# Hyena's three-tap convolution inside the input projection's evictions instead of inside attention

## The reference

```python
def centred_conv3(x, w, b):
    return shift_prev(x) * w[0] + x * w[1] + shift_next(x) * w[2] + b

def hyena(u, sw, sb, ...):
    u = centred_conv3(u, sw, sb)              # per sequence, zero at its ends
    v, x1, x2 = jnp.split(u, 3, axis=-1)
    z = v
    for o, gate in enumerate((x1, x2)):
        conv = ...                            # long convolution with kernel o, by Fourier transforms
        z = gate * (conv + skip[o] * z)
    return z

p = h @ w_in                                  # 3 * 512 columns q, k, v, then 3 * 512 for Hyena
y = concat([attention(q, k, v, kc, vc, rpb), hyena(p[..., 3 * A:], ...)]) @ w_out
```

## Time and profile before

| | us |
|---|---|
| median of 3 runs | 2537.68 (2536.79 to 2539.23) |
| profiled execution, first to last instruction | 2542.4 |
| of it, PE busy | 2305.5 |
| DVE, ACT, POOL busy | 946.4, 664.9, 864.1 |
| first eviction of a Hyena tile to the last (starts) | 194.27 to 315.55 |
| first scores of attention to the last store | 318.67 to 438.05 |

### The profile page before, as it was taken

One profiled execution on the slowest core, in us unless ns is written; L12 is line 12 of the kernel. 1 busy time (PEld: TensorE's weight loads), 2 busy tenths in 40 slices (PEclk: granted clock), 3 DMA queues, 4 the chain that ended last, 5 costly groups with the idle time before them and its releaser, 6 DMA issues. The chain is left out here.

```text
span 2542.4 us, 50323 instructions
## 1 busy us (share of the span) xinstructions
PE 2305.5 (91%) x22240; PEld 1932.1 (76%) x22240; DVE 946.4 (37%) x1475; ACT 664.9 (26%) x1031; POOL 864.1 (34%) x699
## 2 busy tenths in 40 slices
PE   5899976998889999999958998999999987999997
PEld 3787854555479999999927987888888865888785
DVE  3110066793130000022288214677777633000123
ACT  4110065431240000022132123444444223111112
POOL 2222200000224343434306444333333233666562
PEclk8999997998889999999979999999999988999998
DMA  6555520001111212111112343222221112323221
GB/s 255 199 215 199 198 92 18 0 1 58 42 42 59 66 58 66 58 60 65 48 50 69 107 145 86 42 44 42 42 42 40 23 59 83 99 91 99 87 96 67
DMA packets 139266, 204.06 MB, mean 80 GB/s; under 512 B 87783, under 2 KB 97511, under 8 KB 131912
## 3 DMA queue, kind: packets, MB, share of 16 engines
q1 hardware_dynamic: 139080, 201.26, 25.1%
HBM read 183.93 MB, written 17.30 MB: 79 GB/s over the span
## 5 line engine op out<-in xcount | busy, mean ns | idle before, releaser
L258 POOL CAST TMP_r<-WR 128x1024 fp32r<-128x1024 f32 x120 | 126.5, 1054 | 730.2 <-DMA WR<-in_ffn_w_dram 438.3
L277 PE MATMUL PS<-H_r,TMP_r 128*128 128x384 f32 (+1 forms) x1088 | 330.6, 359 | 10.9 <-DVE Y_r L494 10.9
L277 PE MATMUL PS<-Y_r,TMP_r 128*128 128x384 f32 (+1 forms) x1088 | 330.2, 358 | 3.7 <-DVE H_r L494 3.7
L260 POOL TENSOR_TENSOR WR_r<-WR,TMP_r 128x1024 fp32r<-128x1024 f32 x120 | 289.2, 2410 | 9.6
L417 DVE TENSOR_TENSOR P<-TMP,PS 128x768 f32 (+1 forms) x44 | 36.1, 821 | 562.8 <-PE PS L277 562.8
L277 PEld LDWEIGHTS PS<-H_r,TMP_r 128*128 128x128 f32 x1088 | 202.7, 190 | 27.4 <-DVE Y_r L494 11.6
L277 PEld LDWEIGHTS PS<-Y_r,TMP_r 128*128 128x128 f32 x1088 | 201.7, 190 | 19.3 <-DVE H_r L494 4.0
L277 PE MATMUL PS<-H_r,WR_r 128*128 128x384 f32 x736 | 191.9, 342 | 0.0
L400 ACT ACTIVATE TMP<-PS 128x768 f32<-128x768 f32 (+1 forms) x44 | 31.0, 705 | 526.3 <-PE PS L277 526.3
L594 PE MATMUL PS<-H_r,TMP_r 128*128 128x384 f32 x704 | 151.9, 338 | 3.2 <-DVE H_r L632 2.2
L277 PE MATMUL PS<-Y_r,WR_r 128*128 128x512 f32 x352 | 139.4, 396 | 0.0
(11 more groups left out here) (321 smaller groups left out, 4526.1 us busy)
## 6 DMA issues: line engine op xcount, KB each, us to landing
WR<-in_ffn_w_dram SPq DMA_DIRECT2D x88, 512.0 KB, 3.6
TMP<-in_mod_w_dram SPq DMA_DIRECT2D x40, 1024.0 KB, 4.9
WR<-in_down_dram SPq DMA_DIRECT2D x44, 512.0 KB, 3.5
WR<-in_mix_w_in_dram SPq DMA_DIRECT2D x24, 512.0 KB, 7.0
WR<-in_rw_w_rkv_dram SPq DMA_DIRECT2D x24, 512.0 KB, 4.2
P<-in_mod_w_dram SPq DMA_DIRECT2D x4, 2048.0 KB, 21.8
vkr_dram<-extra SPq DMA_DIRECT2D x16, 384.0 KB, 4.8
scan_front<-vkr_dram SPq DMA_DIRECT2D x16, 384.0 KB, 4.2
```

The lines of the kernel that those rows point to most:

```text
L258: nc.gpsimd.tensor_copy(hi, raw).then_inc(weights_hi, 1)
L260: nc.gpsimd.tensor_tensor(lo, raw, hi.bitcast(F32), ALU.subtract).then_inc(weights_split, 1)
L277: last = nc.tensor.matmul(PS[:, bank + b, 0:h1 - h0], w, x[:, h0:h1], start=k + p == 0, stop=k == CT - 1 and p == 2)
```

## The change

The taps are applied where a Hyena tile leaves PSUM. ACT's eviction of tile t (12 to 23) becomes scale by the middle weight plus bias, and counts `conv3_begun`. DVE then adds the left tap and the right tap, reading the neighbours from the PSUM banks, that is the values before any tap, and adding in place to tile t of `P`. The two halves of 384 columns and the border at column 512 cut each tap into three instructions. Only after the second tap does DVE count `inproj.unit_free`. Nothing of the convolution is left in attention or Hyena. The convolved tiles now lie at 12 to 23, so Hyena reads `P[:, HY + ...]` with HY = 12, and `WAVES` moves to tiles 0 to 11.

Two orders change besides. On DVE, `inproj_dve` interleaves the convolutions with the modulation columns. On PE, the scores of steps 0 and 1 begin as soon as bank pairs 0 and 1 are free of their last tiles, and the last turn of the modulation follows them.

```diff
@@ attn_pe
+            for u in range(2):
+                pe.wait_ge(inproj.unit_free, IN_TILES - IN_UNITS + u + 1)
+                scores(u)
+            mod_turn_pe(pe, NMOD - 1)
             pe.wait_ge(inproj.unit_free, inproj.done)
-            scores(0)
-            scores(1)
             pe.wait_ge(mod_added, NMOD)
...
@@ attn_act
-            def conv3_begin(i, j):
-
-                act.wait_ge(scores_done, 2 * (6 * i + 6))
-                act.wait_ge(v_done, 3 * i + 3)
-                nc.scalar.activation(P[:, 4 * j + i, :], P[:, 12 + 4 * j + i, :], ACT.Identity,
-                                     scale=col(SW_COL + 12 + 4 * j + i), bias=col(SB_COL + 4 * j + i))\
-                  .then_inc(conv3_begun, 1)
...
-                if u >= 6 and u % 6 < 3:
-                    conv3_begin(u // 6 - 1, u % 6)
             out(STEPS - 1)
-            for j in range(3):
-                conv3_begin(PAIRS - 1, j)
...
-        def conv3_dve(v, i, j):
-            src, dst = P[:, 12 + 4 * j + i, :], P[:, 4 * j + i, :]
-            for step, (begun, n) in enumerate(((conv3_begun, 3 * i + j + 1), (conv3_step, 3 * i + j + 1))):
-                v.wait_ge(begun, n)
-                for s0, s1, _ in segs():
-                    here, there = (slice(s0 + 1, s1), slice(s0, s1 - 1))[::1 if step == 0 else -1]
-                    ins = nc.vector.scalar_tensor_tensor(dst[:, here], src[:, there],
-                                                         col(SW_COL + 24 * step + 4 * j + i), dst[:, here],
+        def conv3_dve(v, t):
+
+            b = 2 * (t % IN_UNITS)
+            raw = P[:, t, :]
+            steps = (((0, 0, HALF, 1), (1, 0, L - HALF - 1, HALF + 1), (1, L - HALF, HALF - 1, L + 1)),
+                     ((0, 1, HALF, 0), (1, 0, L - HALF, HALF - 1), (1, L - HALF + 1, HALF, L)))
+            for step, parts in enumerate(steps):
+                if step == 0:
+                    v.wait_ge(conv3_begun, t - 11)
+                else:
+                    v.wait_ge(conv3_step, t - 11)
+                for bank, c0, c1, at in parts:
+                    dst = raw[:, at:at + c1 - c0]
+                    ins = nc.vector.scalar_tensor_tensor(dst, PS[:, b + bank, c0:c1], col(SW_COL + 24 * step + t - 12), dst,
                                                          ALU.mult, ALU.add)
-                ins.then_inc(conv3_done if step else conv3_step, 1)
+                ins.then_inc(inproj.unit_free if step else conv3_step, 1)
+
+        def inproj_dve(v, chain):
+            for i in range(2):
+                network_dve(v, chain, 0, i)
+            for g in range(1, 3):
+                mod_cols_dve(v, g)
+                network_dve(v, chain, 1, g - 1)
+            for t in range(12, 17):
+                conv3_dve(v, t)
+            mod_cols_dve(v, 3)
+            for t in range(17, 21):
+                conv3_dve(v, t)
+            mod_cols_dve(v, 4)
+            for t in range(21, IN_TILES):
+                conv3_dve(v, t)
+            mod_cols_dve(v, 5)
...
@@ attn_dve
-                if u >= 6 and u % 6 < 3:
-                    conv3_dve(v, u // 6 - 1, u % 6)
-            conv3_dve(v, PAIRS - 1, 0)
...
-        WAVES, EARLY, LATER = Pf[:, 12 * T:24 * T], WRf, Hraw[:, 4 * T:8 * T]
+        WAVES, EARLY, LATER = Pf[:, 0:12 * T], WRf, Hraw[:, 4 * T:8 * T]
+        HY = 12
...
@@ hyena_pe
             pe.wait_ge(attn_out, STEPS)
-            pe.wait_ge(conv3_done, 10)
             filters(0, 1, 0)
...
@@ hyena_dve
-            v.wait_ge(conv3_done, 10)
-            conv3_dve(v, PAIRS - 1, 1)
             filtered(0, 1, 0)
             filtered(0, 3, 4)
             filtered(0, 0, 2)
-            conv3_dve(v, PAIRS - 1, 2)
             filtered(1, 1, 2)
...
@@ inproj_pe
-            mod_turn_pe(pe, NMOD - 1)
...
@@ inproj_act
-                    nc.scalar.activation(as_halves(P[:, t, :]), halves(b), ACT.Copy).then_inc(inproj.unit_free, 1)
+                    nc.scalar.activation(as_halves(P[:, t, :]), halves(b), ACT.Identity, scale=col(SW_COL + t),
+                                         bias=col(SB_COL + t - 12)).then_inc(conv3_begun, 1)
```

More of the change, by code:

```diff
@@ L691, in hybrid_dit_kernel @@
         conv3_step = sem("conv3_step")
-        conv3_done = sem("conv3_done")
         def latent(u):
@@ L1079, in turn @@
                         pe.wait_ge(HDV.sem, HDV[f"z{r - 2}.{c}"])
-                    last = nc.tensor.transpose(PS[:, bank, 128 * c:128 * c + 128], P[:, c, at:at + 255:2], ident[:, :])
+                    last = nc.tensor.transpose(PS[:, bank, 128 * c:128 * c + 128], P[:, HY + c, at:at + 255:2], ident[:, :])
                 HPE.done(last, f"zt{r}.{k}")
@@ L1426, in gated @@
                 v.wait_ge(HAC.sem, HAC[f"sc{r}.{c}"])
-                tmp, z = scaled_of(r, c), P[:, c, first:first + n]
+                tmp, z = scaled_of(r, c), P[:, HY + c, first:first + n]
                 HDV.done(nc.vector.scalar_tensor_tensor(tmp, z, col(SKIP_COL + 4 * o + c), tmp, ALU.mult, ALU.add),
@@ L1431, in gated @@
                 HDV.done(nc.vector.tensor_tensor(z if o == 0 else H[:, 4 + c, first:first + n], tmp,
-                                                 P[:, 4 + 4 * o + c, first:first + n], ALU.mult), f"z{r}.{c}")
+                                                 P[:, HY + 4 + 4 * o + c, first:first + n], ALU.mult), f"z{r}.{c}")
             def product(r, f):
                 products(nc.vector, HDV, v, r, f, slice(0, HW))
-            v.wait_ge(conv3_done, 10)
-            conv3_dve(v, PAIRS - 1, 1)
             filtered(0, 1, 0)
@@ L3041, in _ @@
                            early=lambda t: Y[:, t, :])
-            for i in range(2):
-                network_dve(v, chain, 0, i)
-            for g in range(1, NMOD):
-                mod_cols_dve(v, g)
-                if g < 3:
-                    network_dve(v, chain, 1, g - 1)
+            inproj_dve(v, chain)
             attn_dve(v)
```

## The result

The changed kernel takes 2500.33 us (median of 4 runs, 2493.22 to 2507.65); the kernel before 2537.23 us (4 runs, 2534.24 to 2539.23: the three above and one more). The ratio is 0.9855, 95% interval 0.9837 to 0.9872: 36.9 us less, where 35.1 were forecast, and 2500.3 us where 2502.6 were. The profiled execution of the changed kernel took 2497.23 us, with a span of 2495.4.

What follows compares the result with a forecast made beforehand. The prediction took PE (91% busy) as the bound, with waits in attention's convolution loops. Savings of 27.9 + 1.4 + 3.3 + 2.7, less 0.2, gave 35.1 us: 2537.7 to 2502.6 us, range 2496 to 2517.

Steps and rivals of the forecast that it cites:

- Part 1: Attention without the convolution: two pairs of heads at 20.0 us each and three loops at 9.1, together 27.9 us saved.
- sixth kind of step: Attention step with queries, scores and values but no batch of values, hidden behind a convolution before; taken as 3.45 us.
- floor of 18.0: Lower bound in us for a pair of heads in attention, from PE's own work, busy 90% in the first pair.
- Part 2: Last three steps of attention: full instead of half clock, 5.0 us in place of 6.4, 1.4 us saved.
- Part 3: From attention to Hyena: PE's filters wait only for the last store, not the tenth convolution; 3.3 us saved.
- Part 4: First Hyena filters: 2.7 us saved if full clock holds through the hand-over, 0 if not.
- Part 5: Input projection: 2.9 us of DVE taps per tile stay hidden; attention's start loses some 0.2 us.
- A: Rival, chance 0.1: attention runs into PE at half clock, each such pair losing 9 us; one gives 2512 us.
- B: Rival, chance 0.06: GpSimd and DVE exclude each other in the projection, and the turn into attention is slow; 2511 us.
- D: Rival, chance 0.02: the convolution in attention was hidden and other waits replace it; 2532 us.
- C: Rival, chance 0.03: evictions hold PE back in the projection from 19.2 us per tile, slower than before from 23 us.
- hidden five times over: Projection: a tile's bank pair is free after some 4.1 us, while PE wants it back only after 19.2 us.

Runs made afterwards that it cites:

- e2: The kernel before with all twelve convolutions left out (wrong result): 2504.40 us, ratio 0.9869.
- e5: The kernel before without ACT's twelve begins of the convolution, DVE's taps left where they are (wrong result): 2510.68 us, ratio 0.9894.
- e9: The changed kernel with three unused ACT instructions put behind attention's last store, PE's filters waiting for them: 2509.24 us in one run.
- e3: The changed kernel without DVE's taps, ACT's eviction freeing the banks: 2501.82 us, ratio 0.9852.
- e6: The changed kernel with the taps reading a tile in SBUF instead of the PSUM banks (wrong result): 2498.42 us in one run.

## Why the prediction was right, step by step

- **Part 1** carries most of the sum and held: pairs of 19.88 and 19.89 us against 20.0, three loops of 9.01 against 9.1, together 28.2 against 27.9. e2 shows that the conv, and nothing else in the change, is its cause. The sixth kind of step, which the trace of before could not show, takes 3.3 us where 3.45 was taken. The warning not to multiply 4.03 by the loops was right, and e5 gives the size: 3.09 us a loop. The floor of 18.0 was too low: the stretch from 335.42 on, from which it was read, holds 158 matmuls and begins at no store, a pair has 170, and PE's work of a pair is 18.34 us. So the pairs stand 1.5 us above their floor.
- **Part 2** had the right mechanism and a wrong size: 3.90 us where 5.0 was taken, 2.5 saved in place of 1.4. At clock 1.00 PE is busy 3.30 of 4.18 us up to the filters, so ACT and DVE end fewer waits than assumed. e2 and e5 support the cause: with gaps of 0.40 and 1.66 us ahead of these steps in place of 3.37 the clock is 1.00.
- **Part 3** held to 0.1 us.
- **Part 4** held in size (2.7). Its reason was incomplete: it makes the 2.7 us depend on whether the clock stays up through the hand-over, and does not see that part 3 removes a gap that brings it down. e9 shows that this gap is enough by itself. Both it and the idle loops were removed, so the sum did not notice; that is luck.
- **Part 5**: taps 2.57 us a tile against 2.9 (the six durations do add up to 2.87; on the engine they overlap a little), ACT 0.99, nothing lost to them (e3). The exclusion was judged rightly from lines 417 and 632 (21 of line 417's 22 instructions of 512 elements ran beside a split, and each took 0.69 us), and e6 shows both sides of it. The 0.2 us at the start lies below what can be told there.
- **Rivals.** A fell: the clock is 1.00 in each pair. Its price of 9 us a pair was too low: the same 38 matmuls kept PE busy 5.82 us at 0.50 and 3.30 at 1.00, by which a whole pair at 0.50 would be some 32 us of PE work (an estimate), 12 us above the 19.9 measured. B's first half is shown by e6 to need other operands; it would have cost nothing here. D fell with the first look at the pairs. **C did not occur, but its working was wrong**, and so was "hidden five times over": the bank pairs don't set the threshold. By 200.4 + 12 D the projection is slowed from between 10 and 11 us of DVE work per tile on (an estimate; no run lies between 7.3 and 13.1), not 19.2, and the change would have been slower than before from some 13 us on, not 23. With 2.6 us there was room for a factor of four, which is why the error did no harm.

What stays open: why the part behind 1300 us differs by up to 12 us between executions. The last eviction of the projection also varies, 309.7 to 316.1 over the runs in which DVE did not hold PE back. Neither depends on the change in any comparison made here, and neither was followed up.

## What to carry to other kernels

Small work of a third engine is not cheap because the engine is idle 60% of the time: look at the loop in which it stands, and price it with a loop of the same trace that lacks it, not with its own duration. Move it to a stage in which its engine waits for tiles, and compare its time per tile with the period of the tiles; spare buffers only put off the moment at which PE waits. Count a gap of some 3 us in front of a PE stage twice, once as waiting and once as slower products behind it, if PE came to it at full clock.

## What the runs showed of the hardware

- A gap of 3.17 us on PE behind stretches at clock 1.00 brought the granted clock to 0.70 in the products that follow; 16 of them took 9.88 us instead of 6.97 (e9). Within the pairs, where PE is busy 92% and its longest wait is 0.6 us, it stayed at 1.00. In the second pair of e5 and in the three conv loops behind it, with waits up to 1.8 us and PE busy 84% and 69%, it was 0.93 and 0.87.
- Six taps over 1532 elements take DVE 2.57 us with one input from PSUM, and up to 5.02 with both from SBUF when a 2.5 us split ran on GpSimd at that time; 2.6 with both from SBUF and nothing beside them (e6). The weight per partition does not count as a second SBUF input.
- ACT's eviction of 768 elements per partition, with a scale and a bias for each partition, takes 0.992 us, the plain copy 0.81.
- The same code from the RWKV projection to the end took 1176.4 us in one execution and 1188.5 in another.
